# Three transformer blocks on one core: squares behind later exponentials, scores in other banks, state-space groups between pairs of gate tiles; last attention heads ahead of late weight halves

## The chip, the cores and the metric

The kernel runs on one NeuronCore of a Trainium2 chip. TensorE (PE) multiplies matrices into eight PSUM banks, VectorE (DVE), ScalarE (ACT) and GpSimd (POOL) work on tiles in SBUF and PSUM, and DMA queues, issued mostly by SyncE (SP), bring weights from HBM. The metric is the device time of one execution in microseconds (us), the median over several; lower is better.

## The reference

The reference chains three blocks on 256 tokens of width 1024, batch 1, all in float32: an mLSTM layer and a differential-attention layer with feed-forward nets; an attention plus state-space block with a product-key expert layer; and a recurrent block. Two pieces matter here.

Differential attention, eight heads. Each has two score maps; with a = softmax(scores) the output is (a0 - lam * a1) @ V, then a norm over the head, then `@ w_out`:

```python
s = jnp.einsum('bhqd,bhkd->bhqk', qi, k_sh)
a = jax.nn.softmax(s, axis=-1).reshape(B, H, 2, Q_BLOCK, S)
diff = a[:, :, 0] - lam * a[:, :, 1]
o = jnp.einsum('bhqk,bhkv->bhqv', diff, v_sh)
o = rms_norm(o, subln) * (1.0 - lam_init)
```

The state-space mixer has 32 heads in 8 groups of 4. Per group g it needs the products C B^T (256 by 256, causal); per head a decay matrix exp(ac_t - ac_s), multiplied into them with dt; then that matrix times the head's x, plus d_skip * x, times silu(z), and a norm over the group's 256 channels (a sum of squares per token). Beside it stand gates, sigmoid of `h @ w_in` columns, called gb here, eight feature tiles of 128.

## The kernel before

**Weights.** Every weight goes through SBUF in chunks of up to 1 MB (`raw`, three slots). A chunk is cut in two pieces. Each piece is split in two halves: the high half is ACT's copy to a rounded format (L2556, `high_to`), the low half DVE's difference (L1361, `low_to`). PE then makes three products per piece, high by high, high by low, low by high. SP loads the next chunk into a slot only when both pieces of the chunk in it have been split. A call `weights()` on ACT or DVE brings the splitting up to a planned piece, `upto`, and then takes some steps of a side program (`go_on`); on PE it takes the steps and waits for the piece. Each engine runs its own instruction list strictly as it was written out, so the order of these calls is the order of the work.

**Two shapes of product.** `features` makes one tile of 128 outputs for 256 tokens per piece: 24 matmuls, lines L533, L534, L537. `down` makes 512-wide products, 12 per piece (L603). The last pieces of a `down` (five here, `LATE`) are kept in spare SBUF and computed at the end for token half 0, then 1.

**Differential attention (`diff`).** Head work goes through stages on the three engines: scores, `mix` (DVE: reciprocals, L1803 to L1812), the turned matrix (PE L837, DVE copy L1778), values (PE L866 to L868, DVE copy L1820, ACT squares L2887), norm (DVE L1825, POOL's power, DVE L1833). `attention(i)` emits the two steps of index i and i + 1, stage q for head i - q. The last three such pairs, i = 6, 8, 10, and the transposes of the output (`out_pair`, PE L890, ACT L2908, DVE L1856) stand inside the output projection `down("df", ...)`: a hook `before(t)` ahead of piece t emits pair 6 at t = 0, pair 8 at t = 2 and pair 10 at t = 3. On ACT and DVE `weights()` for t = 0 and t = 1 therefore split four late pieces between pairs 6 and 8. The pieces of t = 3 to 7 go to spare SBUF (R in the rows); the first piece after them ("halves") belongs to the next feed-forward net and its chunk takes the slot that held t = 2 and 3.

**State space (`mix2`, `ssm`).** Three side programs with the same steps, one per engine. For g = 0 to 10: group g (PE: C B^T, L1034 and L1035; DVE copy L2052), its four decays (PE L1041 to L1043 broadcasts the exponents; ACT exponentials L3041, L3042; DVE multiplies L2060), the sums of group g - 1 (PE L1052 to L1054, 24 matmuls; DVE L2072, L2079; ACT squares L3048), the variance of g - 2 (DVE L2105), the scaling of g - 3 (DVE L2086). That is 64 steps. They are woven into the eight gate tiles `features("m2.gb", 8)`: 28 empty steps, then 14 steps ahead of each tile. So tiles 0 and 1 go first, and then 14 steps stand ahead of each of tiles 2 to 6.

**Banks.** `main` is banks 0 to 3, `aux` banks 4 to 7, each taken in turn. Before the change group, decay and sums all take from `aux`, and the gate tiles from `main`, one bank per two tiles. A take waits until the bank's last content has been read.

Of the kernel before, what the change touches and what calls it, by code (L numbers as in the profile page):

```python
# [95 lines left out]
class On:  # L96
# [13 lines left out]
    def go_on(self):  # L110
        for _ in range(self.steps):
            if self.side is not None and next(self.side, self) is self:
                self.side = None

    def finish(self):
        while self.side is not None:
# [340 lines left out]
def tensor_engine(k):  # L457

    nc, ps, X, d = k.nc, k.ps, k.X, k.d
# [115 lines left out]
    def features(key, nf, act, ready, KT=8, second=None, behind=None, start=0):  # L575
        a = KT if KT == 8 else KT // 2
        if second:
            first = four(key, act, ready, second)
        for f in range(4 if second else start, nf):
            if f % 2 == 0:  # L580
                b = main.take(pe, (key, f))
            o = f % 2 * 256
            for q in range(KT // a):
                n, hi, lo = weights()
                ins = tile_mms(ps[:, b, o:o + 256], n, hi, lo, act, q * a, a, q == 0, q == KT // a - 1, ready)
                ins.then_inc(k.piece_read, 1)
            if f % 2:
                k.full[key, f - 1] = k.piece_read, n + 1
            if (f == 5) if second else (f == 1 and behind):
                turn_back(key, first, ((key, 0), (key, 2))) if second else behind()  # L590
# [356 lines left out]
    def mix2(prev):  # L947
# [81 lines left out]
        pe.finish()  # L1029

        def group(g):
            b = aux.take(pe, ("m2", "cb", g))
            pe.wait_ge(*s["act"].need(("m2.conv", 30)))
            mm(ps[:, b, 0:256], BT[:, g, 0:128], CT[:, g, :], start=True, stop=True)  # L1034
            ins = mm(ps[:, b, 256:384], BT[:, g, 128:256], CT[:, g, 128:256], start=True, stop=True)  # L1035
            filled(("m2", "cb", g), ins)
# [7 lines left out]
            filled(("m2", "L", h), ins)  # L1044

        def sums(g):
            b = aux.take(pe, ("m2", "ssm", g))
            for h in range(4 * g, 4 * g + 4):
                o, L = h % 4 * 64, L_[:, h % 8, :]
                hs = slice(h * 64, h * 64 + 64)  # L1050
                pe.wait_ge(*s["prob"].need(("m2.L", h)))
                mm(ps[:, b, o:o + 64], L[:, 0:128], xs[:, 0, hs], start=True, stop=True)  # L1052
                mm(ps[:, b, 256 + o:320 + o], L[:, 128:256], xs[:, 0, hs], start=True, stop=False)
                ins = mm(ps[:, b, 256 + o:320 + o], L[:, 256:384], xs[:, 1, hs], start=False, stop=True)  # L1054
            filled(("m2", "ssm", g), ins)

        def ssm():
            for _ in range(28):
                yield
            for g in range(11):  # L1060
                if g < 8:
                    group(g)
                    yield
                    for r in range(4):
                        decay(4 * g + r)
                        yield
                if 1 <= g < 9:
                    sums(g - 1)
                    yield
                if 2 <= g < 10:  # L1070
                    yield
                if g >= 3:
                    yield

        pe.begin(ssm(), 14)
        features("m2.gb", 8, X, rx)
        pe.finish()
        turn("m2.n", xs, lambda j: [], n=16, each=lambda c, j: s["chan"].need(("m2", c // 2, j)))
        features("m2.ys", 8, k.pair(8192, 16, lo=19456), turned("m2.n"), KT=16)
# [266 lines left out]
def vector_engine(k):  # L1346
# [149 lines left out]
    def features(evac, key, nf, KT=8, by_four=False):  # L1496
        if by_four:
            for _ in range(4):
                weights()
            split(key)  # L1500
        for f in range(4 if by_four else 0, nf):
            for q in range(1 if KT == 8 else 2):
                weights()
            if by_four and f == 5:
                evac(0)
                evac(2)
            if f % 2:
                evac(f - 1)
# [271 lines left out]
    def diff(prev):  # L1780
# [84 lines left out]
            v.finish()  # L1865

        def before(t):
            for i in {0: (6,), 2: (8,), 3: (10,)}.get(t, ()):
                if i < 10:
                    out_pair(i - 6)  # L1870
                for _ in attention(i):
                    pass
                if i == 10:
                    out_pair(4)
                    out_pair(6)
# [26 lines left out]
    def mix2(prev):  # L1902
# [146 lines left out]

        def group(g):  # L2050
            v.wait_ge(*full["m2", "cb", g])
            te.tensor_copy(cbs[:, g % 2, :], ps[:, aux.of(("m2", "cb", g)), 0:384]) \  # L2052
                .then_inc(*aux.done(("m2", "cb", g)))

        def decay(h):
            L = L_[:, h % 8, :]
            v.wait_ge(*aux.gone(("m2", "L", h)))
            v.wait_ge(*aux.gone(("m2", "cb", h // 4)))
            for j, o in enumerate((slice(0, 256), slice(256, 384))):
                ins = te.scalar_tensor_tensor(L[:, o], L[:, o], cc[:, 32 * j + h:32 * j + h + 1],  # L2060
                                              cbs[:, h // 4 % 2, o], ALU.mult, ALU.mult)
            ins.then_inc(*s["prob"].mark(("m2.L", h)))

        def sums(g):
            gs = slice(g * 256, g * 256 + 256)
            v.wait_ge(*full["m2", "ssm", g])
            v.wait_ge(*k.dma[f"gb{ROW_LOADS.index('misc') % 2}"].need("misc"))
            y = ps[:, aux.of(("m2", "ssm", g)), :].rearrange("p (j c) -> p j c", c=256)
            for q in range(4):
                h = 4 * g + q  # L2070
                hs = slice(h * 64, h * 64 + 64)
                ins = te.scalar_tensor_tensor(xs[:, :, hs], xs[:, :, hs], gv[:, 256 + h:257 + h],  # L2072
                                              y[:, :, q * 64:q * 64 + 64], ALU.mult, ALU.add)
            ins.then_inc(*aux.done(("m2", "ssm", g)))
            if g == 7:
                k.row_read["misc"] = aux.gone(("m2", "ssm", g))
            v.wait_ge(*aux.gone(("m2", "ssm", g)))
            v.wait_ge(*s["gated"].need("m2.z"))
            te.tensor_tensor(xs[:, :, gs], xs[:, :, gs], zz[:, :, gs], ALU.mult).then_inc(*s["part"].mark(("m2.y", g)))  # L2079

# [6 lines left out]
                    .then_inc(*s["chan"].mark(("m2", g, j)))  # L2087

        def ssm():
            for _ in range(28):  # L2090
                yield
            for g in range(11):
                if g < 8:
                    group(g)
                    yield
                    for r in range(4):
                        decay(4 * g + r)
                        yield
                if 1 <= g < 9:
                    sums(g - 1)  # L2100
                    yield
                if 2 <= g < 10:
                    n = 2 * (g - 2)
                    v.wait_ge(*s["square"].need(("m2.y", g - 2)))
                    te.tensor_scalar(cc[:, 128 + n:130 + n], cc[:, 128 + n:130 + n], 1.0 / 256, 1e-6,  # L2105
                                     ALU.mult, ALU.add).then_inc(*s["var"].mark(("m2.g", g - 2)))
                    yield
                if g >= 3:
                    scale(g - 3)
                    yield  # L2110

        v.begin(ssm(), 14)
        features(nothing, "m2.gb", 8)
        v.finish()
        turned("m2.n", k.pair(8192, 16, lo=19456), lambda c: col("sn", c), n=16)
        gB, tt, mx = k.ar(15360, 8, 256), k.ar(2048, 2, 2, 256), k.pair(4096, 8)
# [422 lines left out]
def scalar_engine(k):  # L2539
# [138 lines left out]
    def out_of(key, dst, func=ACT.Copy, scale=1.0):  # L2678

        def evac(f):  # L2680
            a.wait_ge(*full[key, f])
            act(dst[:, f:f + 2, :], two(main.of((key, f))), func, scale=scale) \
                .then_inc(*main.done((key, f)))
        return evac
# [183 lines left out]
    def diff(prev):  # L2868
# [49 lines left out]
            a.finish()  # L2918

        def before(t):  # L2920
            for i in {0: (6,), 2: (8,), 3: (10,)}.get(t, ()):
                if i < 10:
                    out_pair(i - 6)
                for _ in attention(i):
                    pass
                if i == 10:
                    out_pair(4)
                    out_pair(6)
# [21 lines left out]
    def mix2(prev):  # L2950
# [99 lines left out]
            ins.then_inc(*s["square"].mark(("m2.y", g)))  # L3050

        def ssm():
            for _ in range(28):
                yield
            for g in range(11):
                if g < 8:
                    yield
                    for r in range(4):
                        decay(4 * g + r)
                        yield  # L3060
                if 1 <= g < 9:
                    sums(g - 1)
                    yield
                if 2 <= g < 10:
                    yield
                if g >= 3:
                    yield

        gB, tt, mx = k.ar(15360, 8, 256), k.ar(2048, 2, 2, 256), k.pair(4096, 8)
        a.wait_ge(*s["act"].need(("m2.conv", 30)))  # L3070
        a.begin(ssm(), 14)
        features(out_of("m2.gb", gB), "m2.gb", 8)
        a.finish()
        turned("m2.n", k.pair(8192, 16, lo=19456), lambda c: col("sn", c), n=16)
        a.wait_ge(*main.gone(("m2.gb", 6)))
# [425 lines left out]
```

## Time and profile before

| | |
|---|---|
| median of 3 runs | 2941.66 us (2940.91 to 2942.59) |
| the profiled execution | 2941.76 us, of which its span is 2939.9 us |
| busy in the span | PE 98%, PE weight loads 87%, DVE 66%, ACT 56%, POOL 12% |
| granted TensorE clock, mean | 0.989 of full |
| HBM read | 485.36 MB, 166 GB/s |
| instructions | 44447 |

The time of the profiled execution lies 1.9 us above its span and 0.1 us above the median. "Granted clock" is the share of TensorE's full clock that the chip let through; over a short stretch it is 1.0 or 0.5. A row of a timeline gives start, duration, engine, line, operation, output and input, count, and in brackets how long the engine had been idle before it and who ended that. Ends of matmuls are modelled, so the spacing of starts is the better measure of what one costs.

### The profile page before, as it was taken

The page shows a single profiled execution, that of the slowest core. Times are in us where ns is not written, and L with a number is a line of the kernel's source. Part 1 is how long each engine was busy: PE and PEld are TensorE (multiplying, and loading weights), DVE is VectorE, ACT ScalarE, POOL GpSimd, SP SyncE. Part 2 cuts the span into 40 slices and gives each one's busy share as a digit, 9 for nine tenths or more (in the row PEclk, how much of TensorE's full clock was granted, in tenths as well). Part 3 has the DMA queues.
Part 4 walks back from the last instruction along what each step waited for, and adds up shares of the span by engine and source line. Part 5 has one row for each costly group of instructions (what it writes and reads, how often), then busy time and mean ns, then how long its engine had stood idle before and what let it go on. Part 6 is the DMA issues. An engine that isn't in the chain of part 4 may idle for free.

```text
span 2939.9 us, 44447 instructions
## 1 busy us (share of the span) xinstructions
PE 2870.2 (98%) x17894; PEld 2567.0 (87%) x17894; DVE 1951.0 (66%) x3360; ACT 1634.9 (56%) x2792; POOL 341.6 (12%) x309
## 2 busy tenths in 40 slices
PE   7999999899989999999999999999999999999999
PEld 6878888788878877799898999999888889989997
DVE  5656765675566666758665899677555566746775
ACT  5544654664555565456545444777555555655664
POOL 0000000000010002000000343897000000000000
PEclk9999999999999999999899999999999999999999
DMA  6554566456435645346246454434555564536454
GB/s 204 197 169 141 175 195 220 129 188 221 138 115 162 207 165 189 115 135 188 78 129 201 158 187 158 144 130 144 201 187 199 187 235 132 167 92 200 152 181 156
DMA packets 304525, 490.33 MB, mean 167 GB/s; under 512 B 10865, under 2 KB 236529, under 8 KB 295617
## 3 DMA queue, kind: packets, MB, share of 16 engines
q1 hardware_dynamic: 303184, 480.09, 49.6%
q0 software_dynamic: 1136, 7.41, 0.7%
q8 instruction: 143, 2.34, 0.3%
q14 instruction: 62, 0.50, 0.1%
HBM read 485.36 MB, written 2.10 MB: 166 GB/s over the span
## 4 chain that ended last, share of the span: by engine, by line
PE 87%; DVE 7%; ACT 4%; issue 1%; DMA 1%; POOL 0%; SPq 0%; DVEq 0%; POOLq 0%; ACTq 0%
PE ps L603 30%; PE ps L533 11%; PE ps L537 10%; PE ps L534 10%; PE ps L682 10%; PE ps L681 5%; PE ps L1117 2%; DVE halves L1361 2%; PE ps L554 1%; PE ps L1152 1%; DVE XX L1399 1%; ACT XX L2581 1%; ACT AR L2604 1%; DVE R L1361 1%; PE ps L1172 1%
## 5 line engine op out<-in xcount | busy, mean ns | idle before, releaser
L2556 ACT ACTIVATE halves<-raw 128x1024 fp32r<-128x1024 f32 (+1 forms) x842 | 878.4, 1051 | 700.3 <-PE ps L603 334.9
L1361 DVE TENSOR_TENSOR halves<-raw,halves 128x1024 fp32r<-128x1024 f32 (+1 forms) x806 | 965.0, 1218 | 221.7 <-ACT halves L2556 218.9
L533 PE MATMUL ps<-XX,halves 128*128 128x256 f32 (+1 forms) x2360 | 592.0, 288 | 0.0
L534 PE MATMUL ps<-XX,halves 128*128 128x256 f32 (+1 forms) x2360 | 583.1, 284 | 0.0
L603 PE MATMUL ps<-halves,XX 128*128 128x512 f32 x2256 | 525.3, 393 | 5.4 <-DVE XX L1399 2.7
L603 PEld LDWEIGHTS ps<-halves,XX 128*128 128x128 f32 x2256 | 424.1, 189 | 100.7 <-issue 7.9
L533 PEld LDWEIGHTS ps<-XX,halves 128*128 128x128 f32 (+1 forms) x2360 | 455.8, 193 | 2.7 <-issue 2.0
L534 PEld LDWEIGHTS ps<-XX,halves 128*128 128x128 f32 (+1 forms) x2360 | 456.1, 193 | 0.2
L537 PE MATMUL ps<-XX,halves 128*128 128x256 f32 (+1 forms) x2360 | 331.6, 283 | 0.7 <-DVE halves L1361 0.7
L603 PE MATMUL ps<-halves,R 128*128 128x512 f32 x1404 | 322.6, 391 | 0.0
L682 PE MATMUL ps<-XX,halves 128*128 128x512 f32 x1264 | 319.2, 394 | 2.2 <-DVE XX L1399 2.2
L603 PEld LDWEIGHTS ps<-halves,R 128*128 128x128 f32 x1404 | 264.4, 189 | 54.8
L537 PEld LDWEIGHTS ps<-XX,halves 128*128 128x128 f32 (+1 forms) x2360 | 304.6, 192 | 1.2 <-DVE halves L1361 1.1
L682 PEld LDWEIGHTS ps<-XX,halves 128*128 128x128 f32 x1264 | 228.2, 190 | 43.2 <-issue 2.5
L1252 POOL TENSOR_TENSOR st<-st 128x1 f32<-128x1 f32 (+1 forms) x43 | 25.7, 598 | 1539.1 <-DVE st L1426 1316.9
L681 PEld LDWEIGHTS ps<-XX,halves 128*128 128x128 f32 x1264 | 172.6, 191 | 12.6 <-issue 0.3
L681 PE MATMUL ps<-XX,halves 128*128 128x256 f32 x1264 | 176.4, 282 | 0.0
L1376 DVE TENSOR_TENSOR XX<-AR,XX 128x256 fp32r<-128x256 f32 x128 | 54.2, 425 | 142.8 <-ACT XX L3148 142.8
L1331 POOL TENSOR_SCALAR raw<-iota,xsel 128x128 f32<-128x128 f32 x128 | 137.8, 1084 | 36.1 <-PE ps L1117 21.9
L1569 DVE TENSOR_TENSOR AR<-AR,ps 128x256 f32<-128x256 f32 x164 | 68.6, 420 | 83.4 <-ACT AR L2713 83.4
L2713 ACT ACTIVATE AR<-ps 128x256 f32<-128x256 f32 x164 | 61.3, 376 | 88.7 <-PE ps L682 88.7
L1257 POOL TENSOR_TENSOR halves<-raw,halves 128x1024 fp32r<-128x1024 f32 x36 | 92.0, 2557 | 156.9 <-ACT halves L2556 156.9
(368 smaller groups left out, 3539.1 us busy)
## 6 DMA issues: line engine op xcount, KB each, us to landing
raw<-in_w_ffn_in SPq DMA_DIRECT2D x88, 1024.0 KB, 5.2
raw<-in_w_in SPq DMA_DIRECT2D x74, 1024.0 KB, 5.3
raw<-in_uT SPq DMA_DIRECT2D x64, 1024.0 KB, 4.8
raw<-in_peer_v SPq DMA_DIRECT2D x64, 1024.0 KB, 4.9
raw<-in_w_ffn_out SPq DMA_DIRECT2D x44, 1024.0 KB, 4.8
raw<-in_w_up SPq DMA_DIRECT2D x24, 1024.0 KB, 5.8
raw<-in_mlstm_w_in SPq DMA_DIRECT2D x12, 1024.0 KB, 5.3
raw<-in_w_down SPq DMA_DIRECT2D x12, 1024.0 KB, 4.9
```

Source lines behind the costliest of these rows:

```text
L533: mm(o[:, ts], hi[:, q, 0:M], xh[:, k0 + q, ts], start=first and q == 0, stop=False)
L534: mm(o[:, ts], hi[:, q, 0:M], xl[:, k0 + q, ts], start=False, stop=False)
L537: ins = mm(o[:, ts], lo[:, q, 0:M], xh[:, k0 + q, ts], start=False, stop=last and q == a - 1)
L603: ins = mm(ps[:, bs[j * (width // 512) + h], :], xv[:, k0 + t, j * 128:(j + 1) * 128], wv[:, t, h * 512:(h + 1) * 512], start=first and q ...
L681: mm(o[:, 0:256], lo[:, p, :], X[0][:, p, :], start=False, stop=False)
L682: ins = mm(o.rearrange("p (h t) -> p h t", t=256), hi[:, q, :], k.XX[:, :, q, :], start=q == 0, stop=q == 7)
L1257: nc.gpsimd.tensor_tensor(lo, src, hi.bitcast(F32), ALU.subtract).then_inc(k.lo_pool, 1)
L1331: nc.gpsimd.tensor_scalar(OA[:, g % 2, q, :], k.iota[:], ih1[:, 4 * g + q:4 * g + q + 1], gw[:, 4 * g + q:4 * g + q + 1], ALU.is_equal, AL ...
L1361: te.tensor_tensor(lo, src, hi.bitcast(F32), ALU.subtract).then_inc(k.lo_made, 1)
L1569: te.tensor_tensor(dst, dst, o[:, 0:256], ALU.add) \
L2556: act(hi, src, ACT.Copy).then_inc(k.hi_made, 1)
L2713: act((sg if a_ == "g" else hb)[:, f // 2 % 2, g, :], ps[:, k.wide_banks(f).of(tile), 256:512], ACT.Copy) \
```

## The change

Four edits. In `diff`, ACT and DVE emit pair 8, with its `out_pair`, already at t = 0, right behind pair 6; PE's list is as before. In `mix2`, C B^T and the sums take `main` banks; the decays alone keep `aux`. ACT's squares of a group move one step on, behind the exponentials of the group after the next. And the weaving changes: tiles 0 and 1, 22 steps, tiles 2 and 3, 22 steps, tiles 4 and 5, the last 20 steps, tiles 6 and 7. On ACT and DVE a pair of tiles now brings two splits one behind the other, and the first state-space step follows two splits where it followed three on each.

```diff
+    def advance(self, n):
+        for _ in range(n):
+            if next(self.side, self) is self:
+                break
...
         def group(g):
-            b = aux.take(pe, ("m2", "cb", g))
+            b = main.take(pe, ("m2", "cb", g))
...
         def sums(g):
-            b = aux.take(pe, ("m2", "ssm", g))
+            b = main.take(pe, ("m2", "ssm", g))
...
         def ssm():
-            for _ in range(28):
-                yield
...
-        pe.begin(ssm(), 14)
-        features("m2.gb", 8, X, rx)
+        features("m2.gb", 2, X, rx)
+        pe.begin(ssm(), 0)
+        for f in range(2, 8, 2):
+            pe.advance(22)
+            features("m2.gb", f + 2, X, rx, start=f)
         pe.finish()
```

DVE and ACT get the same weaving. In their `diff`, and in ACT's `ssm`:

```diff
         def before(t):
-            for i in {0: (6,), 2: (8,), 3: (10,)}.get(t, ()):
+            for i in {0: (6, 8), 3: (10,)}.get(t, ()):
...
                 if 1 <= g < 9:
-                    sums(g - 1)
                     yield
                 if 2 <= g < 10:
+                    sums(g - 2)
                     yield
```

Line numbers of the changed kernel are 5 to 8 higher (L1367 for L1361). DVE in `diff`, from the norm of head 3 on, before:

```order
489 L1833 TENSOR_SCALAR AR<-AR 128x128 x2
490 L1361 TENSOR_TENSOR R_2048_1154<-raw,R_2048_1154 128x1024
491 L1361 TENSOR_TENSOR R_2048_1156<-raw,R_2048_1156 128x1024
492 L1361 TENSOR_TENSOR R_2048_1158<-raw,R_2048_1158 128x1024
493 L1361 TENSOR_TENSOR R_2048_4627<-raw,R_2048_4627 128x1024
494 L1856 SCALAR_TENSOR_TENSOR R_2048_1990<-ps,cols,R_2048_1988 128x256 x2
495 L1803 RECIPROCAL st<-st 128x2
```

and DVE in the changed kernel, from the same norm, the part in the middle being the rest of pair 8:

```order
489 L1839 TENSOR_SCALAR AR<-AR 128x128 x2
490 L1862 SCALAR_TENSOR_TENSOR R_2048_1990<-ps,cols,R_2048_1988 128x256 x2
491 L1809 RECIPROCAL st<-st 128x2
```

```order
505 L1839 TENSOR_SCALAR AR<-AR 128x128 x2
506 L1367 TENSOR_TENSOR R_2048_1154<-raw,R_2048_1154 128x1024
507 L1367 TENSOR_TENSOR R_2048_1156<-raw,R_2048_1156 128x1024
508 L1367 TENSOR_TENSOR R_2048_1158<-raw,R_2048_1158 128x1024
509 L1367 TENSOR_TENSOR R_2048_4627<-raw,R_2048_4627 128x1024
510 L1367 TENSOR_TENSOR R_2048_1986<-raw,R_2048_1986 128x1024
511 L1367 TENSOR_TENSOR halves<-raw,halves 128x1024
512 L1826 COPY AR<-ps 128x2x128
```

Four splits moved from ahead of pair 8 to behind it, where they join two others; the first of pair 10 (row 512) follows all six, as it did before.

PE in the state-space stretch, from C B^T of group 2 (XX is the turned input, `halves` the weights of a gate tile), before:

```order
2436 L1034 MATMUL ps<-AR 128x256
2437 L1035 MATMUL ps<-AR 128x128
2438 L1041 MATMUL ps<-R_384_8299,sel 128x384
2439 L1042 MATMUL ps<-mask,identb 128x256
2440 L1043 MATMUL ps<-mask,identb 128x128
2441 L1041 MATMUL ps<-R_384_8299,sel 128x384
2442 L1042 MATMUL ps<-mask,identb 128x256
2443 L1043 MATMUL ps<-mask,identb 128x128
2444 L533 MATMUL ps<-XX,halves 128x256
```

and in the changed kernel, from the third decay of that group:

```order
2444 L1046 MATMUL ps<-R_384_8299,sel 128x384
2445 L1047 MATMUL ps<-mask,identb 128x256
2446 L1048 MATMUL ps<-mask,identb 128x128
2447 L1046 MATMUL ps<-R_384_8299,sel 128x384
2448 L1047 MATMUL ps<-mask,identb 128x256
2449 L1048 MATMUL ps<-mask,identb 128x128
2450 L1057 MATMUL ps<-AR 128x64
2451 L1058 MATMUL ps<-AR 128x64
```

Gate tile 2 stood two decays into group 2; now it stands behind the sums of group 1 and three decays of group 3.

## Rows read from the trace of the kernel before

**Rows 1.** The page: engine shares of the chain that ended last.
```profile
PE 87%; DVE 7%; ACT 4%; issue 1%; DMA 1%; POOL 0%; SPq 0%; DVEq 0%; POOLq 0%; ACTq 0%
```

**Rows 2.** Waits of PE, whole span: us in total, times, longest us.
```profile
PE ps L1041 <- DVE AR L2052: 3.6, 5, 1.2
```

**Rows 3.** Windows: length, busy PE, PEld, DVE, ACT, POOL, granted clock, DMA, GB/s.
```profile
1410.00:1490.40 80.40, 74.95 (x466) 67.52 (x464) 52.90 (x143) 37.56 (x108) 5.79 (x8) 0.79 0.14 40
1415.40:1429.00 13.60, 13.42 (x57) 11.60 (x57) 8.92 (x25) 5.45 (x18) 0.00 (x0) 0.50 0.04 10
1429.00:1439.20 10.20, 9.22 (x74) 8.09 (x73) 6.03 (x17) 5.57 (x17) 0.69 (x1) 0.99 0.37 104
853.60:859.10 5.50, 5.45 (x18) 4.70 (x19) 3.98 (x12) 3.29 (x10) 1.39 (x2) 0.50 0.26 79
```

**Rows 4.** Timeline of PE in the state-space stretch.
```profile
1394.65 1.12 PE L537 MATMUL ps<-XX,halves 128*128 128x256 f32 x8
...
1397.53 1.12 PE L537 MATMUL ps<-XX,halves 128*128 128x256 f32 x8
...
1418.22 0.63 PE L1052 MATMUL ps<-AR 128*128 128x64 f32 x2
...
1423.34 1.17 PE L1034 MATMUL ps<-AR 128*128 128x256 f32 x2
...
1463.97 0.60 PE L1034 MATMUL ps<-AR 128*128 128x256 f32 x2
...
1464.55 0.42 PE L1041 MATMUL ps<-R,sel 96*128 96x384 f32 x1
...
1466.22 0.39 PE L1052 MATMUL ps<-AR 128*128 128x64 f32 x2
...
1468.90 0.65 PE L1034 MATMUL ps<-AR 128*128 128x256 f32 x2
```

**Rows 5.** Timeline of DVE in the state-space stretch.
```profile
1451.76 1.11 DVE L2072 SCALAR_TENSOR_TENSOR AR<-AR,ps 128x128 f32<-128x128 f32 x4
...
1455.19 2.72 DVE L2060 SCALAR_TENSOR_TENSOR AR<-AR 128x256 f32<-128x256 f32 x8 [0.53 <-ACT AR L3042]
```

**Rows 6.** Timeline of ACT at the first exponentials.
```profile
1412.09 1.28 ACT L3041 ACT_TABLE_LOAD   x1
1413.38 0.47 ACT L3041 ACTIVATE AR<-ps,AR 128x256 f32<-128x256 f32 x1
...
1414.01 0.48 ACT L3041 ACTIVATE AR<-ps,AR 128x256 f32<-128x256 f32 x1
```

**Rows 7.** Timeline of DVE in differential attention.
```profile
846.20 4.62 DVE L1361 TENSOR_TENSOR R<-raw,R 128x1024 fp32r<-128x1024 f32 x4
850.74 0.86 DVE L1856 SCALAR_TENSOR_TENSOR R<-ps,cols,R 128x256 fp32r<-128x256 f32 x2
...
857.64 1.22 DVE L1361 TENSOR_TENSOR R<-raw,R 128x1024 fp32r<-128x1024 f32 x1
...
860.85 0.42 DVE L1820 COPY AR<-ps 128x256 f32<-128x256 f32 x1 [0.85 <-PE ps L868]
```

**Rows 8.** Timeline of PE in differential attention.
```profile
846.68 0.60 PE L890 MATMUL ps<-ident,AR 128*128 128x128 f32 x4
...
853.65 0.87 PE L837 MATMUL ps<-ident,AR 128*128 128x128 f32 x3 [5.38 <-DVE AR L1812]
...
863.76 13.87 PE L603 MATMUL ps<-R,R 128*128 128x512 f32 x60
```

**Rows 9.** Timeline of ACT in differential attention.
```profile
849.40 0.81 ACT L2908 ACTIVATE R<-ps,cols 128x256 fp32r<-128x256 f32 x2
...
857.05 1.99 ACT L2556 ACTIVATE halves<-raw 128x1024 fp32r<-128x1024 f32 x2
```

**Rows 10.** Timeline of SP in differential attention.
```profile
847.44 0.37 SPq L1232 DMA_DIRECT2D raw<-in_w_ffn_in  x1
```

**Rows 11.** Landing times of the five weight loads issued from 840 to 870 us.
```profile
DMA to landing us min/median/max: 4.9/5.1/5.8
```

More of the change, by code:

```diff
@@ L2051, in group @@
             v.wait_ge(*full["m2", "cb", g])
-            te.tensor_copy(cbs[:, g % 2, :], ps[:, aux.of(("m2", "cb", g)), 0:384]) \
-                .then_inc(*aux.done(("m2", "cb", g)))
+            te.tensor_copy(cbs[:, g % 2, :], ps[:, main.of(("m2", "cb", g)), 0:384]) \
+                .then_inc(*main.done(("m2", "cb", g)))
         def decay(h):
@@ L2057, in decay @@
             v.wait_ge(*aux.gone(("m2", "L", h)))
-            v.wait_ge(*aux.gone(("m2", "cb", h // 4)))
+            v.wait_ge(*main.gone(("m2", "cb", h // 4)))
             for j, o in enumerate((slice(0, 256), slice(256, 384))):
@@ L2067, in sums @@
             v.wait_ge(*k.dma[f"gb{ROW_LOADS.index('misc') % 2}"].need("misc"))
-            y = ps[:, aux.of(("m2", "ssm", g)), :].rearrange("p (j c) -> p j c", c=256)
+            y = ps[:, main.of(("m2", "ssm", g)), :].rearrange("p (j c) -> p j c", c=256)
             for q in range(4):
@@ L2073, in sums @@
                                               y[:, :, q * 64:q * 64 + 64], ALU.mult, ALU.add)
-            ins.then_inc(*aux.done(("m2", "ssm", g)))
+            ins.then_inc(*main.done(("m2", "ssm", g)))
             if g == 7:
-                k.row_read["misc"] = aux.gone(("m2", "ssm", g))
-            v.wait_ge(*aux.gone(("m2", "ssm", g)))
+                k.row_read["misc"] = main.gone(("m2", "ssm", g))
+            v.wait_ge(*main.gone(("m2", "ssm", g)))
             v.wait_ge(*s["gated"].need("m2.z"))
@@ L2089, in ssm @@
         def ssm():
-            for _ in range(28):
-                yield
             for g in range(11):
@@ L2110, in ssm @@
                     yield
-        v.begin(ssm(), 14)
-        features(nothing, "m2.gb", 8)
+        features(nothing, "m2.gb", 2)
+        v.begin(ssm(), 0)
+        for f in range(2, 8, 2):
+            v.advance(22)
+            features(nothing, "m2.gb", 2)
         v.finish()
@@ L2920, in before @@
         def before(t):
-            for i in {0: (6,), 2: (8,), 3: (10,)}.get(t, ()):
+            for i in {0: (6, 8), 3: (10,)}.get(t, ()):
                 if i < 10:
@@ L3052, in ssm @@
         def ssm():
-            for _ in range(28):
-                yield
             for g in range(11):
@@ L3070, in mix2 @@
         a.wait_ge(*s["act"].need(("m2.conv", 30)))
-        a.begin(ssm(), 14)
-        features(out_of("m2.gb", gB), "m2.gb", 8)
+        features(out_of("m2.gb", gB), "m2.gb", 2)
+        a.begin(ssm(), 0)
+        for f in range(2, 8, 2):
+            a.advance(22)
+            features(out_of("m2.gb", gB), "m2.gb", f + 2, first=f)
         a.finish()
```

## The prediction

> **What bounds the kernel now.** I read the page first: PE is busy 98% of the span and carries 87% of the chain that ended last [rows 1]. So a change pays where PE waits or runs at a lower clock, and nowhere else. Then the waits of PE, which show the two edited places, the windows over them for the granted clock, and last the timelines of each engine there.
>
> State space, 1410.0 to 1490.4 us. The reader is to see 80.40 us, PE busy 74.95, a mean granted clock of 0.79 [rows 3]. Its levels are 1.0 and 0.5, 2.4 and 1.2 GHz. Then (1 - 0.79) / 0.5 * 80.4 = 33.8 us are at the lower level. The first such piece is 1415.4 to 1429.0, 13.6 us; the others share 20.2 us.
>
> What PE would need at the full clock comes from spacings [rows 4]. A gate tile is 1397.53 - 1394.65 = 2.88 us. C B^T is 1464.55 - 1463.97 = 0.58. Four decays are 1466.22 - 1464.55 = 1.67, so 0.42 each. One group's sums are 1468.90 - 1466.22 = 2.68; at the lower level they take 1423.34 - 1418.22 = 5.12, 1.9 times as long. The stretch holds six tiles (17.3), eight C B^T (4.6), 32 decays (13.4) and eight sums (21.4): 56.7 us. So 23.7 us are lost: idle 80.4 - 75.0 = 5.4; the clock 33.8 * (1 - 1 / 1.9) = 16.0; and 2.3 in short gaps that the modelled ends cover.
>
> Why the clock falls: from 1429.0 to 1439.2 PE is busy 9.22 of 10.20 us, so about 1.0 us of waits was followed by a fall [rows 3]. All of PE's decays that wait for DVE's copy, 3.6 us in five waits, are waits for a bank [rows 2]: in `aux`, C B^T holds the bank that the fourth decay behind it takes. The rise at 1429.0 came while a gate tile ran, although PE had been busy 13.42 of the 13.60 us before with sums and decays. I take it that tiles bring the clock back and sums do not.
>
> Differential attention, 846 to 864 us. DVE splits four late pieces for 4.62 us (846.20), and only then does its `out_pair` (850.74) and the mix of head 7 [rows 7]. PE waits 5.38 us for that mix, until 853.65 [rows 8]. It is the longest wait in either place.
>
> **The attention edit.** PE's list is unchanged. It ends the four transposes at 846.68 + 0.60 = 847.28 [rows 8]. ACT, with its four splits gone, does its part (0.81) at once [rows 9], so DVE can start `out_pair` at about 848.2 in place of 850.74, 2.5 us sooner. Mix 7 and PE's turn come 2.5 us sooner too: the wait shrinks from 5.4 to 2.9 us.
>
> What is late next is what was queued behind. From `out_pair` to the first split behind pair 8 DVE takes 857.64 - 850.74 = 6.90 us [rows 7], now 848.2 to 855.1. Then five spare-SBUF splits at 4.62 / 4 = 1.15: 860.9. The sixth is a piece of the next net, and its chunk goes into the slot of t = 2 and 3. SP issued that load at 847.44, as the first of the four splits ended [rows 10]. That split is now the first behind pair 8 and ends at 856.3, so the load lands 5.1 us later [rows 11], at 861.4. Behind it: ACT's split (1.99 / 2 = 1.0, [rows 9]) to 862.4 and DVE's (1.2) to 863.7. Only now comes pair 10, whose first DVE copy stood at 860.85 [rows 7]. It is 2.8 us late, and so is the run of 60 late products, which stood 2.91 us behind the copy, at 863.76 [rows 8]. DVE's work is the same; it stands idle 2.0 us ahead of `out_pair` and 1.6 for the load, in place of 0.85.
>
> PE meanwhile finishes t = 2 and the values of head 7 and idles some 6 us ahead of the 60 products. Behind the wait of 5.38 us PE ran 5.5 us at 0.50 [rows 3], 2.7 us lost; there this lay beside DVE's work, and now it would not. I take half of it, 1.4, with 0 and 2.7 as ends. The sum is +4.2 us. Its ends: +5.5, and -2.5 if DVE's later work turned out to hide.
>
> **The state-space edits.** Start: ACT and DVE have one split less ahead, so the table load stands at 1411.1 in place of 1412.09. The fourth decay needs no bank of C B^T. But decays 5 to 8 now take the banks that exponentials free: the first at 1412.3 + 0.6, the rest 0.63 apart [rows 6], against PE's 0.42. PE waits about 0.4, three times 0.2, and 0.5 for DVE's fourth multiply: 1.5 us in all. The first sums start near 1416.0 in place of 1418.22 [rows 4]. That is still more than the 1.0 us behind which a fall came, so I keep the first fall, near 1415.4.
>
> Then the weaving tells against the change. Still ahead of the next gate tile stand two sums, two C B^T and seven decays: 5.4 + 1.2 + 2.9 = 9.5 us at the full clock, 18.1 at the lower, 8.6 lost. Some 2.2 more go with the tile in which the clock comes back. The first fall costs 10.8 us in place of 13.6 * (1 - 1 / 1.9) = 6.4.
>
> The second block of 22 steps: PE's work per group is 0.58 + 1.67 + 2.68 = 4.9 us. DVE's is 1455.19 + 2.72 - 1451.76 = 6.15 less the wait of 0.53, 5.6 [rows 5]; the wait is what the moved squares remove, since the exponentials no longer stand behind them. Over 22 steps (2.75 groups) and two tiles PE has 13.5 + 5.8 = 19.3 us, DVE 15.4 + 2.4 = 17.8. DVE starts the block ahead, because PE was slow in the first, so I expect no wait there. At the end of the third PE catches up with DVE: about 1.0 us ahead of the last sums, and a fall whose length is a third of 20.2, 6.7 us, or 3.2 lost.
>
> Sum: 56.7 + idle 2.5 + gaps 2.3 + clock 10.8 + 3.2 = 75.5 in place of 80.4, -4.9 us. The later squares cost nothing of their own: DVE's variance of that group stands behind four multiplies (2.72) and a group's sums, ACT's squares only behind four exponentials (4 * 0.63 = 2.5) [rows 5, 6]. Ends: if the first fall stays away, 56.7 + 2.5 + 2.3 + 3.2 = 64.7, -15.7; if the second block falls too, about 9 us of its work at the full clock runs at half, 8.1 + 2.2 = +10.3, so +5.4.
>
> **Together.** -4.9 + 4.2 = -0.7 us on the profiled execution's 2941.76 (span 2939.9 and 1.9 around it), 0.1 above the median: 2941.0 us.
>
> **Rivals.** A: the first fall stays away. For it: the new waits, 1.5 us over some 3.2 us, are five small ones parted by work, and the waits for a bank held by C B^T, up to 1.2 us long [rows 2], are gone. Against it: 1.0 us was enough elsewhere. It gives 2941.7 - 15.7 + 4.2 = 2930.2. The Trainium skill has a rule that goes this way, in "TensorE: Matmul & The Clock Gate", section "A second HAM failure mode: psum-queue depth-cycling": where PE cycles through PSUM banks and "micro-idles between MM groups frequently enough", its clock swings. By that rule parting the banks would be the remedy and A the outcome; the bank waits of [rows 2] agree, but the waits that stay here are for exponentials.
>
> B: the attention edit pays what it seems to. Pair 10's lateness hides, and PE keeps the 2.5 us. For it: PE's wait there is the long one. Against: every later start goes by DVE's order. It gives 2941.7 - 4.9 - 2.5 = 2934.3.
>
> C, slower: the second block of 22 steps, with no tile in it, also runs at the lower level. Place: groups 3 to 6. Price +10.3, so 2941.0 + 10.3 = 2951.3. It decides as soon as PE waits some 1.0 us in that block while DVE is behind; DVE needs 5.6 a group against PE's 4.9, which speaks for it, and its head start against.
>
> D: the change does not do what it says: the waits change their releasers and keep their ends, since DVE's and ACT's work is the same in sum. It gives 2941.7.
>
> **How the numbers follow.** This kernel's measurement tells 0.2%, 5.9 us, from no change. Forecast 52%, with 2936 to 2947 as its own range; A 22%; B 10%; C 12%; D 4%. Faster by over 0.2% (below 2935.8): A, most of B, 4 of the forecast: 0.34. Slower (above 2947.6): C and 2 of the forecast: 0.14. Same: 0.52. The range, 2928 to 2949, takes in A and the near side of C.
>
> **What would show it.** In attention: PE's wait for L1818 near 2.9 us; the load behind the first late split issued near 856.3; the 60 products starting near 866.6 with PE idle some 6 us before. In state space: first sums near 4 us + 12 from its start, one stretch of 0.50 of about 24 us in place of 13.6, no wait of a decay for the copy of C B^T, one short fall late. I am wrong if the 60 products start no later than before, if the clock in the first block holds, or if a second long stretch of 0.50 follows.

## The result, and the profile after

| | before | changed |
|---|---|---|
| median, us | 2941.93 (2940.91 to 2943.01, 5 runs) | 2925.86 (2923.26 to 2928.52, 5 runs) |
| ratio, 95% interval | | 0.9947 [0.9935, 0.9959] |
| profiled execution, us | 2941.76 | 2925.86 |
| its span, mean granted clock | 2939.9, 0.989 | 2924.1, 0.993 |
| busy PE / DVE / ACT | 2870.2 / 1951.0 / 1634.9 | 2855.8 / 1951.1 / 1633.9 |

The change is worth 16.1 us; the forecast said 0.7, and its range ended at 2928. Executions over 1.5% longer than the fastest of their kernel are left out, here and below: one each in runs 1 and 2 of the experiments, two in run 10. DVE and ACT do the same work for the same time, and PE, with the same 17894 instructions, is 14.4 us less busy. Instructions that are the same and take less time point at the clock. The chain line of the page [rows 1] hardly moves:

```profile
PE 88%; DVE 6%; ACT 3%; DMA 1%; issue 1%; POOL 0%; SPq 0%; DVEq 0%; POOLq 0%; ACTq 0%
```

**State space.** The windows of the changed kernel, with the columns of [rows 3]: the whole stretch, its first 8.84 us, and two windows of the attention part.

```profile
1415.78:1474.00 58.22, 58.13 (x466) 53.29 (x464) 51.06 (x142) 36.75 (x107) 5.79 (x8) 1.00 0.19 55
1415.78:1424.62 8.84, 8.75 (x62) 6.91 (x61) 6.96 (x18) 7.48 (x19) 0.00 (x0) 1.00 0.42 120
851.80:857.20 5.40, 5.40 (x21) 4.50 (x22) 3.88 (x12) 3.33 (x11) 1.39 (x2) 0.68 0.02 5
867.10:882.10 15.00, 15.00 (x63) 12.31 (x63) 8.59 (x14) 6.22 (x13) 1.11 (x2) 0.92 0.46 144
```

The clock column reads 1.00 where it read 0.79, and PE is busy all the time. PE's timeline in the first block (start, length, line and form) shows the waits that are left:

```profile
1415.78 0.60 PE L1039 MATMUL ps<-AR 128*128 128x256 f32 x2
...
1417.60 0.42 PE L1046 MATMUL ps<-R,sel 96*128 96x384 f32 x1
...
1418.04 0.65 PE L1039 MATMUL ps<-AR 128*128 128x256 f32 x2
...
1418.99 0.44 PE L1046 MATMUL ps<-R,sel 96*128 96x384 f32 x1
...
1419.62 0.45 PE L1046 MATMUL ps<-R,sel 96*128 96x384 f32 x1
...
1420.86 0.44 PE L1046 MATMUL ps<-R,sel 96*128 96x384 f32 x1
...
1421.32 0.39 PE L1057 MATMUL ps<-AR 128*128 128x64 f32 x2
...
1474.92 3.69 PE L519 MATMUL ps<-ident,AR 128*128 128x128 f32 x32 [0.89 <-ACT AR L2689]
```

The first four decays run through, and C B^T follows the fourth at once. The fifth starts 0.95 us behind it in place of 0.58, and the next three follow 0.62 to 0.63 apart in place of 0.42: some 1.0 us of waiting in small pieces, most of which the modelled ends count as busy. The sums follow the last decay. No wait of a decay for DVE's copy is left; before had 3.6 us of them [rows 2]. From the first C B^T to the 32 transposes behind the stretch it is 1474.92 - 1415.78 = 59.14 us; before, from 1410.01 to 1490.84, it was 80.83. So the stretch gave 21.7 us, and 5.8 were lost ahead of it.

**Attention.** The same places as [rows 7 to 10]: PE, DVE, ACT and SP of the changed kernel.

```profile
847.33 0.60 PE L895 MATMUL ps<-ident,AR 128*128 128x128 f32 x4
...
851.77 0.52 PE L842 MATMUL ps<-ident,AR 128*128 128x128 f32 x3 [2.83 <-DVE AR L1818]
...
865.87 0.69 PE L895 MATMUL ps<-ident,AR 128*128 128x128 f32 x2 [7.26 <-DVE AR L1839]
...
867.18 14.97 PE L608 MATMUL ps<-R,R 128*128 128x512 f32 x60
```
```profile
855.76 5.76 DVE L1367 TENSOR_TENSOR R<-raw,R 128x1024 fp32r<-128x1024 f32 x5
863.14 1.23 DVE L1367 TENSOR_TENSOR halves<-raw,halves 128x1024 fp32r<-128x1024 f32 x1 [1.61 <-ACT halves L2563]
864.28 0.42 DVE L1826 COPY AR<-ps 128x256 f32<-128x256 f32 x1
```
```profile
862.05 2.00 ACT L2563 ACTIVATE halves<-raw 128x1024 fp32r<-128x1024 f32 x2 [3.00 <-DMA raw<-in_w_ffn_in]
```
```profile
857.01 4.91 SPq L1238 DMA_DIRECT2D raw<-in_w_ffn_in  x3
```

PE's wait for the mix of head 7 is 2.83 us in place of 5.38, and a new wait of 7.26 stands ahead of the products. DVE's late splits, now behind pair 8, set when SP issues the next load (857.01); ACT waits 3.00 us for it, DVE 1.61 for ACT. The products start 19.85 us behind PE's four transposes, before 17.08, and take 1.1 us more at a mean clock of 0.92. To the transposes behind them (L491; L486 before) it is 43.37 us from 847.33, before 39.47 from 846.68: +3.9. Some 0.65 us stood ahead of this, and 1.2 come behind it: 286 products start 1119.43 in 66.37 us where before took 65.14, with a piece at a mean of 0.76 (1119.50 to 1125.00). Neither of these two is shown to be the edit's. PE's four transposes start anywhere from 846.03 (run 8 below) to 848.70 (run 1), and in run 2, with the same edit, the 286 products take 65.17 us.

### The profile page after: what moved, and what is told of

The parts are those of the page before. It is cut to its first block, busy times and chain, and to the rows that moved or that the text cites. A ratio compares the mean times of both kernels' runs of the same rounds, so it can differ in the third digit from the quotient of the medians.

```text
span 2924.1 us, 44449 instructions
## 1 busy us (share of the span) xinstructions
PE 2855.8 (98%) x17894; PEld 2554.0 (87%) x17894; DVE 1951.1 (67%) x3360; ACT 1633.9 (56%) x2792; POOL 341.2 (12%) x309
## 4 chain that ended last, share of the span: by engine, by line
PE 88%; DVE 6%; ACT 3%; DMA 1%; issue 1%; POOL 0%; SPq 0%; DVEq 0%; POOLq 0%; ACTq 0%
PE ps L608 30%; PE ps L538 11%; PE ps L542 11%; PE ps L539 10%; PE ps L687 10%; PE ps L686 5%; PE ps L1123 2%; DVE halves L1367 2%; PE ps L559 1%; DVE XX L1405 1%; PE ps L1158 1%; ACT XX L2588 1%; ACT AR L2611 1%; PE ps L1178 1%; PE ps L491 1%
## 5 line engine op out<-in xcount | busy, mean ns | idle before, releaser
L1367 DVE TENSOR_TENSOR halves<-raw,halves 128x1024 fp32r<-128x1024 f32 (+1 forms) x806 | 965.2, 1219 | 224.3 <-ACT halves L2563 221.6
```

Source lines behind the costliest of these rows:

```text
L1367: te.tensor_tensor(lo, src, hi.bitcast(F32), ALU.subtract).then_inc(k.lo_made, 1)
```

## The experiments

"Run" and a number is an experiment here, and "the kernel before" is timed anew beside each group of them (2941.85, 2942.18 and 2941.90 us). The ratios are against it.

**1. The state-space edits alone.** The attention edit is undone:
```
-            for i in {0: (6, 8), 3: (10,)}.get(t, ()):
+            for i in {0: (6,), 2: (8,), 3: (10,)}.get(t, ()):
```


> The changed kernel with the attention edit undone; the state-space edits stay. Theory W (PE's waits, and the clock that follows them, decide the state-space stretch; the attention edit costs): the stretch stays at about 59 us at a granted clock of 1.00, and the attention part ends some 5 us sooner than in the changed kernel: 2941.9 - 21.5 = 2920.5 us. Rival N (the attention edit is neutral, and the whole 16 us come from the state-space edits): 2925.9 us.

Measured: 2922.23 us, 0.9932 [0.992, 0.9945]. That is 3.6 us below the changed kernel, so W's side. The stretch is at 1.00 again.

**2. The attention edit alone**, the reverse edit on the kernel before:

> The kernel before with the attention edit alone. Theory W: the 60 late products start 2.8 us later and run partly at the lower clock, so the next feed-forward net starts about 5 us later: 2941.9 + 5 = 2947 us, the state-space stretch still 80 us at 0.79. Rival N: 2942 us. Rival B of the prediction (PE keeps the 2.5 us): 2939.5 us.

Measured: 2942.59 us, 1.0003 [0.9994, 1.0012]. Two timelines of PE, around the products and around the stretch, say why:

```profile
867.73 15.31 PE L603 MATMUL ps<-R,R 128*128 128x512 f32 x60
...
891.58 1.06 PE L486 MATMUL ps<-ident,AR 128*128 128x128 f32 x8 [0.82 <-ACT AR L2612]
...
1415.46 0.60 PE L1034 MATMUL ps<-AR 128*128 128x256 f32 x2
...
1492.92 3.68 PE L514 MATMUL ps<-ident,AR 128*128 128x128 f32 x32 [0.89 <-ACT AR L2682]
```

PE's four transposes stand at 847.82 here. To 891.58 it is 43.76 us against 39.47: the edit costs 4.3 us at its place. But the state-space stretch is 77.46 us long in place of 80.83, with nothing in it edited: its mean clock is 0.82 in place of 0.79 in this execution. So in this execution the neutral time is a loss of some 4 us and a gain of 3.4 in a stretch that the edit does not touch; by its time alone, N would have won. The other nine have no trace, and why the edit should make the later falls shorter in them too is not shown. In the changed kernel, where the profiled stretch has no fall left to vary, the loss shows (2925.86 with it, 2922.23 without).

**3. Without the new banks**: run 1, with C B^T and the sums back in `aux`.
```
-            b = main.take(pe, ("m2", "cb", g))
+            b = aux.take(pe, ("m2", "cb", g))
```
(and the same for "ssm", on PE and DVE)

> As the first of these, but C B^T and the sums take aux banks again; weaving and squares as in the change. Theory W: decays wait for DVE's copy again, some 8 us of waits in the stretch, the clock falls in blocks that hold no gate tile and stays down longer than before the change: the stretch takes 90 us or more, 2941.9 + 10 = 2952 us, with 2945 to 2960. Rival G (weaving in pairs is what gains, the banks add little): 2921 to 2926 us.

Measured: 2927.35 us, 0.9951 [0.9936, 0.9965]. PE's waits, two of them in the second block, the end of the stretch, and the window over it:
```profile
PE ps L1046 <- DVE AR L2058: 4.6, 5, 1.1
```
```profile
1439.71 0.44 PE L1046 MATMUL ps<-R,sel 96*128 96x384 f32 x1 [1.12 <-DVE AR L2058]
...
1446.01 0.44 PE L1046 MATMUL ps<-R,sel 96*128 96x384 f32 x1 [1.11 <-DVE AR L2058]
...
1475.72 3.69 PE L519 MATMUL ps<-ident,AR 128*128 128x128 f32 x32 [0.89 <-ACT AR L2689]
```
```profile
1410.52:1474.83 64.31, 58.92 (x466) 53.19 (x464) 51.98 (x143) 37.29 (x107) 5.79 (x8) 1.00 0.18 50
```
The waits for the copy are all there, even longer in sum than before (4.6 against 3.6), and the clock holds. W's 2952 us is far off, and G's upper end, 2926, is nearly met. The stretch takes 65.20 us to the transposes, 6.1 more than in run 1. PE is idle 5.4 us in its window, 4.6 of it for the copy and 0.8 for an exponential, where run 1 has next to nothing. So the kernel is 5 us slower than run 1 by the waits themselves, and not by the falls that I had put behind them.

**4. Without the later squares**: run 1 with ACT's `sums(g - 1)` back in its old place.

> As the first of these, but ACT's squares stand where they stood before. Theory W: with no wait of PE left in the stretch, DVE being about 0.5 us per group later still fits: no change against the first, 2920.5 us. Rival Q (the later squares are needed): DVE falls behind PE in the second block, waits appear, the clock falls: 2930 us.

Measured: 2920.90 us, 0.9934 [0.9919, 0.9948], and the same 59.14 us from the first C B^T (1411.69) to the transposes (1470.83). Beside the other two edits the later squares do nothing to the middle. But of its four times (2919.40, 2919.84, 2921.97 and 2926.73) one lies 4.8 us above the next, at a mean clock of 0.993 where the others have 0.995 and 0.996. It has no trace. So it is open whether that execution had a fall in the stretch or elsewhere.

The next four ask what in the weaving holds the clock. **5. The weaving alone**, on the kernel before (old banks, old squares):
```
-        features("m2.gb", 8, X, rx)
+        features("m2.gb", 2, X, rx)
+        pe.begin(ssm(), 0)
+        for f in range(2, 8, 2):
+            pe.advance(22)
+            features("m2.gb", f + 2, X, rx, start=f)
```


> The kernel before with nothing but the new weaving: two tiles, 22 steps of the state space, two tiles, and so on; C B^T and the sums stay in their old banks and the squares where they were. Theory P (the weaving alone ends the clock falls; the banks take the waits away; the squares do nothing): the clock holds 1.00 in the stretch, five waits of decays for DVE's copy of 4 to 5 us in all stay, the stretch is 65 us long, 2926 to 2928 us. Rival Q (the old squares delay the exponentials, and with the bank waits beside them that is enough for a fall): at least one piece of 0.50 in the stretch, 2932 us or more.

Measured: 2930.78 us, 0.9962 [0.9945, 0.998], but five runs from 2926.14 to 2945.42. The profiled one was the slowest of them and had three pieces at 0.50 in the stretch, so Q came true there. The fastest, at a mean clock of 0.996, fits P, but has no trace.

**6. The early start alone**: the kernel before, in which ACT and DVE begin the state space one split sooner, in the old rhythm.
```
-        v.begin(ssm(), 14)
-        features(nothing, "m2.gb", 8)
+        features(nothing, "m2.gb", 2)
+        v.begin(ssm(), 0)
+        for f in range(2, 8):
+            v.advance(14)
+            weights()
```


> The kernel before, with one thing changed: ACT and DVE begin the state space right behind the splits of the second gate tile, one split sooner than before; the old rhythm of 14 steps and one tile stays, as do banks and squares. PE's order is that of before. Theory P (the fall of the first block comes from ACT and DVE starting late: their waits of 0.59 and 0.94 us stand close together there): the first stretch at 0.50 goes away (6.4 us), the later ones stay or move: 2933 to 2937 us. Rival T (the rhythm decides, the start does not): the same falls as before, 2940 to 2943 us.

Measured: 2934.96 us (2932.43 to 2940.75, 8 runs), 0.9974 [0.9964, 0.9984]. That is P's price, 7 us. The diff is DVE's; ACT has the same. Windows of the kernel before and of this one, each over the first 5.39 us of the stretch:
```profile
1410.01:1415.40 5.39, 3.86 (x25) 2.62 (x23) 3.80 (x7) 5.36 (x11) 0.00 (x0) 1.00 0.59 171
```
```profile
1412.98:1418.37 5.39, 4.59 (x30) 3.13 (x29) 3.61 (x9) 5.36 (x13) 0.00 (x0) 1.00 0.60 174
```
Before, PE stood still for 1.53 of these 5.39 us, and the fall followed at once. With the early start it is 0.80. The profiled execution, the slowest of the eight, still fell, but 9.0 us behind its start, and three more times later. So that the first fall is what went away in the others is argued from their times, not seen.

**7. A late start in the changed kernel**: run 1, with one split more ahead of the first step on ACT and DVE.
```
         features(nothing, "m2.gb", 2)
+        low_to(k.upto[v.cur] - 1)
         v.begin(ssm(), 0)
```
(and `high_to` on ACT)

> The changed kernel without its attention edit, but with one split more ahead of the first state-space step on ACT and on DVE, as in the kernel before. Theory P (the late start makes the fall, and the long block of 22 steps keeps the clock down until the next tiles): PE waits some 1.2 us for an exponential among the first eight decays, the clock falls to 0.50 in the first block, and it costs about 10 us: 2931 to 2935 us. Rival T (the new rhythm and banks hold the clock whatever the start): one wait of some 1.2 us and no fall, 2923 to 2924.5 us.

Measured: 2921.68 us, 0.9931 [0.9914, 0.9948]. The wait is there, in one piece, and the clock is not touched:
```profile
1413.33 0.44 PE L1046 MATMUL ps<-R,sel 96*128 96x384 f32 x1 [1.03 <-ACT AR L3050]
```
```profile
1409.18:1468.37 59.19, 58.16 (x466) 53.29 (x464) 51.09 (x142) 36.73 (x107) 5.80 (x8) 1.00 0.19 55
```
T was right: here a single wait of 1.03 us, beside three small ones of 0.2, is followed by no fall, and the four times lie within 2.2 us. That is no rule for single waits, as the account below shows.

**8. Pair 8 of the attention one step earlier than before**, not two: run 1 with
```
-            for i in {0: (6,), 2: (8,), 3: (10,)}.get(t, ()):
+            for i in {0: (6,), 1: (8,), 3: (10,)}.get(t, ()):
```


> The changed kernel, but pair 8 of the differential attention ahead of the second step (t = 1) on ACT and DVE, where before had it ahead of the third and the change ahead of the first. Two of the four splits then stand before pair 8 and two behind it. Theory P (DVE's idle time is what is gained or lost: it has work while ACT and PE get ready, and the load behind the first late split starts earlier than in the changed kernel): PE's wait for the mix of head 7 near 4 us or less, the 60 products start 0 to 1.5 us earlier than with the attention edit undone, 2920.5 to 2922.5 us. Rival (any split behind pair 8 delays pair 10 as the edit itself did): 2923 to 2926 us.

Measured: 2922.37 us, 0.9932 [0.9916, 0.9947], no better than run 1. PE's timeline and the window over the 60 products, and the same window of the kernel before:
```profile
846.03 0.60 PE L895 MATMUL ps<-ident,AR 128*128 128x128 f32 x4
...
850.74 0.52 PE L842 MATMUL ps<-ident,AR 128*128 128x128 f32 x3 [3.12 <-DVE AR L1818]
...
860.86 0.53 PE L895 MATMUL ps<-ident,AR 128*128 128x128 f32 x2 [3.29 <-DVE AR L1839]
...
862.18 15.37 PE L608 MATMUL ps<-R,R 128*128 128x512 f32 x60
```
```profile
862.10:877.50 15.40, 15.40 (x64) 12.56 (x64) 8.59 (x14) 6.22 (x13) 1.12 (x2) 0.90 0.50 161
```
```profile
863.76:877.60 13.84, 13.84 (x63) 11.43 (x63) 8.51 (x14) 6.22 (x13) 1.12 (x2) 1.00 0.47 152
```
Theory P's times came: the products start 16.15 us behind the transposes, 0.9 sooner than before (17.08). They then take 15.37 us in place of 13.87, at a mean clock of 0.90, and the gain is gone. Run 1's trace is as before here (16.93 and 13.87 us). The lower clock stands behind the second wait, which grew from 1.20 to 3.29 us; that it comes from that wait is not tried by itself.

The last four ran on one chip, to see the spread. **9. Run 3 again:**

> The kernel of the run without the bank change (new weaving, later squares, no attention edit), beside the next one on one chip. In it the decays wait 4.6 us for DVE's copy, and its four times lay within 1.5 us. Theory V (such waits make the clock a matter of chance, with the squares at either place): times spread over 10 us or more, from 2926 up to some 2940 us, on a chip where the weaving alone does so too. Rival W (the later squares keep the clock up): all runs within 2925 to 2929 us.

Measured: 2926.90 us (2925.07 to 2934.21, 7 runs), 0.9957 [0.9943, 0.9972].

**10. Run 5 again:**

> The weaving alone again, with the old squares and banks. Theory V: times from 2926 to 2945 us as in its first runs, and no different in the middle from the run beside it with the later squares. Rival W: its middle lies 3 us or more above that run, and its fastest runs (2926 us) are those in which no fall happened.

Measured: 2931.81 us (2927.74 to 2940.04, 6 runs), 0.9967 [0.9953, 0.9981]. The spread is V's, but the middle is W's: run 9 lies 5 us lower, and only one of the eleven runs of that kernel (3 and 9 together) is above 2928. Windows of run 9, then of run 10, over the first 8.84 us of the stretch and the 14 us behind:
```profile
1409.76:1418.60 8.84, 7.31 (x52) 5.52 (x50) 6.96 (x18) 7.60 (x19) 0.00 (x0) 1.00 0.42 120
1418.60:1433.00 14.40, 13.88 (x112) 12.72 (x111) 12.06 (x31) 7.54 (x21) 0.70 (x1) 1.00 0.01 2
```
```profile
1415.36:1424.20 8.84, 7.31 (x52) 5.52 (x50) 6.96 (x18) 7.59 (x19) 0.00 (x0) 1.00 0.42 120
1424.40:1438.80 14.40, 14.40 (x64) 12.31 (x64) 7.72 (x23) 5.14 (x19) 0.69 (x1) 0.53 0.00 0
```
The first rows of both are equal in every engine, to 0.01 us. The second rows are 1.00 and 0.53: the same 8.84 us of work with the same 1.53 us of waits stand ahead, and in one execution the clock falls. The two kernels differ only in ACT's squares, which come later than these 8.84 us in both. PE's decays further on in run 10 show how the clock comes back, and two waits of which one is followed by a fall (at 1451.7) and one is not:
```profile
1450.31 0.44 PE L1046 MATMUL ps<-R,sel 96*128 96x384 f32 x1 [1.11 <-DVE AR L2058]
...
1457.99 0.67 PE L1046 MATMUL ps<-R,sel 96*128 96x384 f32 x1
...
1458.64 0.42 PE L1046 MATMUL ps<-R,sel 96*128 96x384 f32 x1
...
1475.66 0.44 PE L1046 MATMUL ps<-R,sel 96*128 96x384 f32 x1 [1.11 <-DVE AR L2058]
```

**11. The later squares alone**, on the kernel before:
```
-                    sums(g - 1)
                     yield
                 if 2 <= g < 10:
+                    sums(g - 2)
```


> The kernel before with the later squares alone. Theory V (the squares do nothing, beside or without bank waits): 2941 to 2943 us, and the same pieces of 0.50 in the stretch. Rival W (the later squares shorten ACT's waits and so take away falls): the wait of 0.40 us of the sums for an exponential is gone, one fall fewer, 2935 to 2939 us.

Measured: 2937.43 us (2928.27 to 2939.34, 12 runs), 0.9985 [0.9975, 0.9995]: W. The window in which before fell for the second time (1439.2) holds here, and the wait of 0.40 us of the sums for an exponential is gone:
```profile
1430.00:1452.00 22.00, 20.20 (x161) 17.90 (x160) 16.82 (x49) 13.61 (x42) 2.15 (x3) 1.00 0.17 49
```
The other three falls of before are still in the trace. From the first C B^T (1410.47) to the transposes (1487.15) it is 76.68 us.

**12. Run 1 again, as control:**

> The state-space edits whole, no attention edit, beside the other three on one chip. With no bank waits of the decays there is no fall in the stretch: 2921 to 2924 us in every run, a spread under 4 us, whatever the chip. If a run lies 5 us or more above the others, the falls can come without the bank waits too.

Measured: 2921.98 us (2920.19 to 2923.00, 6 runs), 0.9938 [0.9924, 0.9952]. The stretch is 59.14 us to the hundredth, as in the changed kernel and in runs 1 and 4:
```profile
1411.33:1469.58 58.25, 58.16 (x466) 53.29 (x464) 51.09 (x142) 36.75 (x107) 5.79 (x8) 1.00 0.20 55
```

What the runs say together, by kernel:

| kernel | idle PE in the first 8.84 us | median | highest less lowest |
|---|---|---|---|
| run 12 (banks, weaving, squares) | 0.1 (same work as the changed kernel) | 2921.98 | 2.8 |
| run 9 (weaving, squares) | 1.5 | 2926.90 | 9.1 |
| run 10 (weaving) | 1.5 | 2931.81 | 12.3 |
| before, beside them, 20 runs | 1.7, of it 1.5 in 5.4 us | 2941.90 | 11.9 |

The some 1.0 us of small waits in the first block of run 12 is spacing, as in the changed kernel, and not in its 0.1. The last column holds for these runs only: run 3, the kernel of run 9, had 1.5 us in four executions, and run 4, with no wait for a bank, 7.3 in four.

The banks alone were not tried: as I read the order, in the old rhythm a gate tile holds a bank of `main` over 14 steps, and C B^T would wait there for a bank that is freed only behind it.

## Why the prediction was wrong

**Base and views: right.** PE at 98%, the stretch at 0.79, 56.7 us of work at the full clock. The stretch without falls takes 58.22 us up to its last wait (58.25 in run 12), 1.5 above the 56.7.

**The failed step: "That is still more than the 1.0 us behind which a fall came, so I keep the first fall".** It carried the term of 10.8 us, and the measured one is 0. What failed in it is the price put on waits, the step from their sum to a fall. The sum of waits was too high: PE's sums wait head by head, so DVE's fourth multiply (0.5 us) is waited for by nobody, and the rest came to some 1.0. And I took one fall behind 1.0 us of waits as a rule, where runs 9 and 10 show that 1.53 us in 8.84 are followed by a fall or not. Single waits are no surer. A lone wait of 1.0 to 1.2 us is followed by a fall within 3 us in 10 of 19 places in all the traces: twice in before (1454.72 and 1472.07), once of two in run 10 (above), in none of six in runs 3 and 9, not in run 7. The two of 0.59 and 0.94 within 5.39 us are followed by one in each of the three traces that have them (before, runs 2 and 11).

```profile
1454.72 0.44 PE L1041 MATMUL ps<-R,sel 96*128 96x384 f32 x1 [1.16 <-DVE AR L2052]
...
1472.07 0.44 PE L1041 MATMUL ps<-R,sel 96*128 96x384 f32 x1 [1.11 <-DVE AR L2052]
```

What the runs show in place of the step is that behind four waits of 0.2 to 0.4 us no fall came in any of the five traces that have only those, nor in run 7. Rival A, at 22%, named this ground, small waits parted by work. Its time of 2930.2 is nearer than its sum deserves: its stretch of 64.7 us is 6.5 too long, by the two terms it kept, below, and by 2.3 of other waits and gaps that shrank, and against that 1.6 more than it said were lost ahead of the stretch.

**The tiles.** The 10.8 also rests on "I take it that tiles bring the clock back and sums do not". No fall in the changed kernel tried it, but run 10 does: its clock rose at 1438.0 and at 1458.5, both times in decays, with no gate tile since the falls at 1424.4 and 1451.7. So in these two places the clock came back without one. And the 13.6 us of [rows 3] hold 2.9 us of a tile already (PE's L533 from 1426.13), beside sums and decays.

**The late fall, 3.2 us, and the wait of 1.0 ahead of the last sums: neither came.** I had let PE catch up with DVE at the end of the third block; it did not, and over the stretch DVE is busy 51.06 of 58.22 us against PE's 58.13, so the slack lay with DVE. So of the forecast's 75.5 us the clock's 14.0 are gone, and of idle and gaps (4.8) 1.5 are left. The forecast's -4.9 is -21.7 by the trace.

**The banks, the weaving and the squares** were taken as one sum. The runs part them. The waits for a bank cost their own 5 us in the time (6.1 in the stretch, 59.14 against 65.20 us in run 3) and, beside it, falls come with them in some executions. With all of them in place run 3's stretch is still 15.6 us shorter than before, so the greater part of the 21.7 is the weaving and the squares. The start one split sooner is worth 7 us alone (run 6). The weaving whole is worth 10 to 11 alone (runs 10 and 5), with much chance in it. The squares, costed at nothing, are worth nothing in the changed kernel (run 4), as said, but 4.5 us on the kernel before (run 11), where the wait of 0.40 beside one of 0.59 went and with it, in the trace, the second fall. The gains do not add; as I read it, each removes some of the same falls.

**Attention: right.** +4.2 was forecast and +3.9 (changed kernel) and +4.3 (run 2) measured between the same landmarks. The wait of 2.9 is 2.83; the load, forecast at 861.4, came for ACT at 862.05, 0.65 of it the offset; the products, forecast at 866.6, stand at 867.18; the clock's part, 1.4, is 1.1. PE stands still 7.26 us, not some 6, and that changes nothing. Rival B, the gain of 2.5 kept, is out by these traces, although run 2 timed alone would not have shown the loss: in its trace shorter falls 550 us later hid it.

**Rival C, a longer second fall, is out; D too.** That DVE needs more per group than PE did not decide, since DVE was ahead when the block began: there it waited 1.33 us for ACT and 1.03 for PE (1438.13 and 1439.91 in the changed kernel).

**The rule of the Trainium skill**, in "TensorE: Matmul & The Clock Gate", section "A second HAM failure mode: psum-queue depth-cycling", on PE that "micro-idles between MM groups frequently enough" went the way of rival A. Run 3 shows 4.6 us of bank waits with the clock at 1.00, and run 10 shows the first two waits of that kernel, 0.80 and 0.74 us, with 0.53 behind them; without such waits none of the six profiles (the changed kernel, runs 1, 4, 7, 8 and 12) has a fall in the stretch. So the traces agree with the rule as a risk, and not as a certainty.

**What stays open.** Why the weaving shortens or removes falls while the waits for a bank stay is not shown: run 6 has the early start alone, but no run has the pairs of tiles without it. Which of two executions with the same waits falls is not settled. Nor is why the old squares (run 10) bring longer times so much more often than the later ones (run 9), while the profiled fall in run 10 begins where PE, ACT and DVE have done the same work. The profiled executions of runs 5, 6 and 10 were the slowest of their kernels, so their traces show the worst case and not the usual one.

## What to carry to other kernels

Where PE's granted clock falls in a stretch, look at PE's waits ahead of each fall. Here they came to 4.9 us in the stretch (3.6 for the copy, 0.9 and 0.4 for exponentials), and the edits against them gave 21.7. Don't carry a fall over to a new order of work because its waits have the same sum; the same waits were followed by a fall in one execution and not in another, so give both outcomes a chance, and let the range hold both ends. Time a kernel several times, since one trace shows one outcome. And read an edit's trace at its own landmarks beside its time: a loss of 4 us did not show in the time of the kernel before, and did in the changed one.

## What the runs showed of the hardware

- The clock's fall does not follow from the program alone. Two executions with 7.31 us of busy PE in the first 8.84, on every engine alike to 0.01 us, went on at 1.00 and at 0.53 (runs 9 and 10), and one kernel took from 2927.74 us at a mean clock of 0.994 to 2940.04 at 0.989 (run 10).
- A narrow spread of times does not tell that there are no falls. Run 2 has three in its trace, and its ten times lie within 3.4 us; the kernels of runs 5, 6, 9, 10 and 11 spread over 8 to 19 us.
- The clock came back from 0.50 to 1.00 while PE was busy nearly all the time: in before all four times in a gate tile (the first at 1429.0, 13.42 of 13.60 us busy), in run 10 twice in decays (1438.0 and 1458.5).
- A gain in waits can be lost again in clock: in run 8, two waits of 3.12 and 3.29 us in place of one of 5.38 and one of 1.2 stand with 60 products that start 0.9 us sooner and take 1.5 us longer, at 0.90.
